# A third seven-product unit in the gate/up chunks of a macaron hybrid layer, with two low parts formed by an adding DMA

## The reference, cut to what matters

```python
def _swiglu_ffn(x, norm_g, w_gate, w_up, w_down):
    h = _rmsnorm(x, norm_g)
    return (jax.nn.silu(h @ w_gate) * (h @ w_up)) @ w_down

h = h + 0.5 * _swiglu_ffn(h, ffn1_norm[l], ffn1_w_gate[l], ffn1_w_up[l], ffn1_w_down[l])
...
h = h + 0.5 * _swiglu_ffn(h, ffn2_norm[l], ffn2_w_gate[l], ffn2_w_up[l], ffn2_w_down[l])
```

## Time and profile before

| | |
|---|---|
| three runs | 2593.53, 2599.84 and 2605.59 us |
| median | 2599.84 us |
| span of the profiled execution | 2591.4 us |
| TensorE busy in the span | 2562.1 us, 99% |
| VectorE, ScalarE, GpSimd busy | 75%, 52%, 7% |
| mean of DMA share and rate | 67% of 16 engines, 212 GB/s |

### The profile page before, as it was taken

The page is one execution under the profiler, slowest core; times in us unless marked ns, Lnnn a source line. Parts: engine busy times, 40 slices in busy tenths (PEclk is TensorE's granted clock), DMA queues, the critical chain, the costliest instruction groups (busy, mean ns, idle before and its releaser), DMA issues.

```text
span 2591.4 us, 34224 instructions
## 1 busy us (share of the span) xinstructions
PE 2562.1 (99%) x13659; PEld 2103.4 (81%) x13659; DVE 1954.8 (75%) x2311; ACT 1339.8 (52%) x1568; POOL 189.2 (7%) x346
## 2 busy tenths in 40 slices
PE   8999999999999999999999999999999999999998
PEld 7888888888888777878788888888888888888887
DVE  6888888887767796959666766555668888888876
ACT  5555555555556366446455544433455455555554
POOL 2000000000000011010001112000100000000000
PEclk9999999999999999999999999999999999999999
DMA  6767676667776575656488779643767677766655
GB/s 213 232 210 242 210 236 218 217 208 228 216 210 195 184 228 159 179 165 181 146 280 257 252 245 281 201 155 130 239 190 230 222 226 225 227 219 218 210 201 175
DMA packets 278576, 548.21 MB, mean 212 GB/s; under 512 B 25020, under 2 KB 35424, under 8 KB 278032
## 3 DMA queue, kind: packets, MB, share of 16 engines
q1 hardware_dynamic: 253904, 478.60, 58.3%
q0 software_dynamic: 24192, 66.89, 8.8%
q10 hardware_dynamic: 320, 0.53, 0.1%
HBM read 508.15 MB, written 37.77 MB: 211 GB/s over the span
## 4 chain that ended last, share of the span: by engine, by line
PE 86%; DVE 8%; ACT 3%; DMA 2%; issue 1%; POOL 0%; SPq 0%; DVEq 0%; ACTq 0%; POOLq 0%
PE pp L794 14%; PE pp L795 14%; PE pp L796 14%; PE pp L415 11%; PE pp L416 11%; PE pp L417 11%; DVE wlo L376 2%; PE pa L794 1%; PE pb L796 1%; PE pb L795 1%; PE pb L794 1%; PE pa L795 1%; PE pa L796 1%; ACT whi L371 1%; DMA raw<-in_ffn_w_up 1%
## 5 line engine op out<-in xcount | busy, mean ns | idle before, releaser
L376 DVE TENSOR_TENSOR wlo<-raw,whi 128x1024 fp32r<-128x1024 f32 (+1 forms) x764 | 919.6, 1216 | 345.9 <-ACT whi L371 326.2
L371 ACT ACTIVATE whi<-raw 128x1024 fp32r<-128x1024 f32 (+1 forms) x764 | 798.0, 1053 | 626.5 <-PE pp L417 438.1
L794 PE MATMUL pp<-whi,xhi 128*128 128x512 f32 x1040 | 404.6, 389 | 0.0
L795 PE MATMUL pp<-whi,xlo 128*128 128x512 f32 x1040 | 404.6, 389 | 0.0
L796 PE MATMUL pp<-wlo,xhi 128*128 128x512 f32 x1040 | 404.6, 389 | 0.0
L415 PE MATMUL pp<-whi,xhi 128*128 128x512 f32 (+1 forms) x928 | 370.6, 399 | 0.7 <-DVE xlo L533 0.7
L417 PE MATMUL pp<-wlo,xhi 128*128 128x512 f32 (+1 forms) x928 | 359.6, 388 | 0.1
L416 PE MATMUL pp<-whi,xlo 128*128 128x512 f32 (+1 forms) x928 | 359.6, 387 | 0.0
L847 ACT ACTIVATE whi<-tw 128x1024 fp32r<-128x1024 f32 x124 | 131.6, 1062 | 276.3 <-PE pp L796 131.6
L794 PEld LDWEIGHTS pp<-whi,xhi 128*128 128x128 f32 x1040 | 195.2, 188 | 40.7
L796 PEld LDWEIGHTS pp<-wlo,xhi 128*128 128x128 f32 x1040 | 195.2, 188 | 40.6
(11 more groups left out here) (528 smaller groups left out, 3669.7 us busy)
## 6 DMA issues: line engine op xcount, KB each, us to landing
raw<-in_ffn_w_gate SPq DMA_DIRECT2D x176, 512.0 KB, 4.3
raw<-in_ffn_w_up SPq DMA_DIRECT2D x176, 512.0 KB, 4.7
raw<-in_ffn_w_down SPq DMA_DIRECT2D x176, 512.0 KB, 4.6
raw<-in_w_in SPq DMA_DIRECT2D x144, 512.0 KB, 4.3
hid_dram<-hid_t POOLq DMA_DIRECT2D x43, 512.0 KB, 5.0
xq<-hid_dram POOLq DMA_DIRECT2D x156, 128.0 KB, 3.8
raw<-in_w_lift SPq DMA_DIRECT2D x32, 512.0 KB, 5.9
raw<-in_w_out SPq DMA_DIRECT2D x32, 512.0 KB, 5.1
```

What stands on the lines that cost most here:

```text
L371: nc.scalar.activation(whi[:, s, :, 0:width], raw[:, r % RING, :, 0:width], ACT.Copy).then_inc(whi_ready, 1)
L376: nc.vector.tensor_tensor(wlo[:, s, :, 0:width], raw[:, r % RING, :, 0:width], whi[:, s, :, 0:width].bitcast(F32), ALU.subtract).then_inc( ...
L794: nc.tensor.matmul(out, a_hi, whi[:, s, block, :], start=start, stop=False)
L795: nc.tensor.matmul(out, a_lo, whi[:, s, block, :], start=False, stop=False)
```

## The change

`GU_UNITS, GU_AFTER` becomes a table for each chunk, `GU_PLAN`. Chunks 1 to 9 get three units instead of two (row blocks 6, 7 and 5, behind t = 1, 3 and 5), so `na` is 5 instead of 6 and there are 10 plain slots instead of 12. Chunk 10 keeps two units behind t = 1 and 5. The third field names plain slots whose low part VectorE no longer writes (t = 1 and 9; in chunk 10 t = 1, 5 and 9): ScalarE writes the negated weights' copy, rounded as `whi` is, to `wlo` (`negate_hi`), and POOL then issues a DMA which reads the weights from DRAM a second time and adds them onto `wlo` (`move_lo`). TensorE waits for the landing of that DMA (`wait_moved`). The sums of activations that a third unit needs are formed once for f1 and once for f2 during chunk 0 (`whole_x`, `xs_third`). Three semaphores are merged with others to make room for two new ones.

```diff
-GU_UNITS, GU_AFTER = (6, 7), (1, 5)
+GU_PLAN = {i: ((6, 7, 5), (1, 3, 5), (1, 9)) for i in range(1, NFC - 1)}
+GU_PLAN[NFC - 1] = ((6, 7), (1, 5), (1, 5, 9))
...
+def copied_at(units, after):
+
+    return max(KT // SK - len(units), after[-1] + 1)
...
         def raw_free(sp, r):
             if r >= RING:
-                sp.wait_ge(wlo_ready, freed_by[r - RING] + 1)
+                last = freed_by[r - RING]
+                if last in lo_moved:
+                    sp.wait_ge(sem("acts_ready"), ACTS[negated_by[last]])
+                else:
+                    sp.wait_ge(wlo_ready, last + 1)
...
+        def negate_hi(act, w):
+
+            r = raw_of[w]
+            nc.scalar.activation(wlo[:, w % RING, :, :], raw[:, r % RING, :, :], ACT.Copy, scale=-1.0).then_inc(sem("acts_ready"), 1)
+
+        def move_lo(pool, w, source):
+
+            pool.wait_ge(sem("acts_ready"), ACTS[negated_by[w]])
+            nc.gpsimd.dma_start(wlo[:, w % RING, :, :], source, accum_op=ALU.add).then_inc(low_landed(lo_moved[w])[0], 16)
...
-        def hidden_turns(pool, tag):
+        def hidden_turns(pool, tag, w_gate, w_up):
             pool.wait_ge(sem("sums_ready"), SUMS[tag, "x"])
-            for i in range(NFC):
-                hidden_out(pool, tag, i)
+            for i in SEVEN:
+                plain, by_dma = prods[tag + "gu"][2 * i]["pair"]["plain"], GU_PLAN[i][2]
+                for t in by_dma:
+                    pr, j, w, _ = plain[t]
+                    weights = w_gate if pr is prods[tag + "gu"][2 * i] else w_up
+                    move_lo(pool, w, weights[j * SK * P:(j + 1) * SK * P, i * CW:(i + 1) * CW].rearrange("(k p) n -> p k n", p=P))
+                    if t == by_dma[0]:
+                        hidden_out(pool, tag, i - 1)
+            hidden_out(pool, tag, NFC - 1)
...
-            pe.wait_ge(wlo_ready, n + 1)
+            if n in lo_moved:
+                wait_moved(pe, n)
+            else:
+                pe.wait_ge(wlo_ready, n + 1)
...
+                if j == 7:
+                    forms_hi(act, xs_third[:, :, :, :], xshi_third[:, :, :, :], (tag, "x", "third"))
...
                     split_hi(act, w, 0)
-                    if t in GU_AFTER:
-                        unit_act(act, pair, GU_AFTER.index(t), (tag, "gu", i))
-                    if t == pair["na"]:
+                    if w in lo_moved:
+                        negate_hi(act, w)
+                    if t in pair["after"]:
+                        unit_act(act, pair, pair["after"].index(t), (tag, "gu", i))
+                    if t == copied_at(pair["units"], pair["after"]):
...
+                if j == 6:
+                    dve.wait_ge(hi_ready, turns[tag + "norm"][1] + 3)
+                    dve.wait_ge(x_ready, turns[tag + "norm"][1] + 3)
+                    link(dve, v.tensor_tensor(whole_x[:, :, :], xhi[:, 10:12, :].bitcast(F32), xlo[:, 10:12, :].bitcast(F32), ALU.add))
+                    forms(dve, whole_x, xs_third, (tag, "x", "third"))
...
-                    split_lo(dve, w, 0)
+                    if w not in lo_moved:
+                        split_lo(dve, w, 0)
...
-                    if t == pair["na"] + 5:
+                    if t == min(pair["na"] + 5, 2 * pair["na"] - 1):
...
-            pe.wait_ge(consts_ready, 1)
+            pe.wait_ge(ident_ready, 2)
```

More of the change, by code:

```diff
@@ L136, in plan @@
     state = dict(p=0, slot=0, raw=0, t=0, s=0, n=0, d=0, freed=[0, 0])
-    raw_of, freed_by = {}, {}
+    raw_of, freed_by, lo_moved = {}, {}, {}
     last = [None, None]
@@ L153, in unit_slots, with pair_slots @@
         return w, r
-    def pair_slots(a, b, units, after):
+    def pair_slots(a, b, units, after, by_dma=()):
         js = [j for j in range(a["ns"]) if j not in units]
@@ L160, in pair_slots @@
             pair["plain"].append((pr, j, *plain_slot()))
+            if t in by_dma:
+                w = pair["plain"][-1][2]
+                lo_moved[w] = len(lo_moved)
             if t < len(js):
@@ L204, in ffn @@
         turned(tag + "act", NFC, by_pe=0)
-        products(tag + "gu", 2 * NFC, [KT], ups=nats[tag + "act"], seven=lambda i: (GU_UNITS, GU_AFTER) if i in SEVEN else None)
+        products(tag + "gu", 2 * NFC, [KT], ups=nats[tag + "act"], seven=lambda i: GU_PLAN.get(i))
         products(tag + "dn", NDC, [FT], seven=lambda q: (DN_UNITS[tag][q], DN_AFTER[tag][q]))
@@ L226, in plan @@
     ffn("f2")
-    return prods, turns, nats, moved, raw_of, freed_by
+    return prods, turns, nats, moved, raw_of, freed_by, lo_moved
+def copied_at(units, after):
+    return max(KT // SK - len(units), after[-1] + 1)
 def count_marks():
@@ L233, in count_marks @@
     for tag in ("f1", "f2"):
-        sums.append((tag, "x"))
-        acts.append((tag, "x"))
-        banks.append((tag, "x"))
+        for marks in (sums, acts, banks):
+            marks += [(tag, "x"), (tag, "x", "third")]
         for i in SEVEN:
-            for u in GU_UNITS:
-                sums += [(tag, "gu", i, u, step) for step in (1, 2, 3)]
-            acts += [(tag, "gu", i, "copied"), (tag, "gu", i, "gate")]
+            units, after, by_dma = GU_PLAN[i]
+            na = KT // SK - len(units)
+            sums += [(tag, "gu", i, u, step) for u in units for step in (1, 2, 3)]
+            for t in range(2 * na):
+                if t in by_dma:
+                    acts.append((tag, "gu", i, "negated", t))
+                if t == copied_at(units, after):
+                    acts.append((tag, "gu", i, "copied"))
+                if t == na + 4:
+                    acts.append((tag, "gu", i, "gate"))
             banks.append((tag, "gu", i))
@@ L256, in build @@
 def build(nc, A):
-    prods, turns, nats, moved, raw_of, freed_by = plan()
+    prods, turns, nats, moved, raw_of, freed_by, lo_moved = plan()
     SUMS, ACTS, BANKS = count_marks()
+    negated_by = {prods[tag + "gu"][2 * i]["pair"]["plain"][t][2]: (tag, "gu", i, "negated", t)
+                  for tag in ("f1", "f2") for i in SEVEN for t in GU_PLAN[i][2]}
     with ExitStack() as ctx:
@@ L921, in ffn_pe @@
                     plain_pe(pe, pair, t, (xhi, xlo))
-                    if t in GU_AFTER:
-                        n = GU_AFTER.index(t)
+                    if t in pair["after"]:
+                        n = pair["after"].index(t)
                         if n == 0:
-                            pe.wait_ge(sem("banks_free"), BANKS[tag, "x"] if i == SEVEN[0] else BANKS[tag, "gu", i - 1])
-                        unit_pe(pe, pair, n, (xhi, xlo), (xshi, xslo), n)
+                            pe.wait_ge(sem("banks_free"), BANKS[tag, "x", "third"] if i == SEVEN[0] else BANKS[tag, "gu", i - 1])
+                        if n < 2:
+                            unit_pe(pe, pair, n, (xhi, xlo), (xshi, xslo), n)
+                        else:
+                            unit_pe(pe, pair, n, (xhi, xlo), (xshi_third, xslo_third), 0)
             pe.wait_ge(x_ready, s0 + NFC - 1)
@@ L1060, in ffn_dve @@
                 for t, (_, _, w, _) in enumerate(pair["plain"]):
-                    split_lo(dve, w, 0)
+                    if w not in lo_moved:
+                        split_lo(dve, w, 0)
                     if t == 3:
                         nat_turn(dve, None, nats[tag + "act"] + i - 1)
-                    if t in GU_AFTER:
-                        n = GU_AFTER.index(t)
+                    if t in pair["after"]:
+                        n = pair["after"].index(t)
                         if n == 0 and i == SEVEN[0]:
-                            dve.wait_ge(sem("banks_free"), BANKS[tag, "x"])
+                            dve.wait_ge(sem("banks_free"), BANKS[tag, "x", "third"])
                         unit_dve(dve, pair, n, (tag, "gu", i), between=(lambda: gated(i - 1)) if n == 0 else None)
```

35 lines of the change are left out of this document (23 added, 12 removed).

## The result

The changed kernel takes **2788.72 us** (median; 2788.32 to 2794.16), the kernel before 2597.57 in the same measurement: a ratio of **1.074** (95% interval 1.072 to 1.076), or +191 us. The forecast was +55, with a range up to 2700. The direction was right; the size was not, and the time lies outside the range.

What follows compares the result with a forecast made beforehand. TensorE, busy 99% of the span, was taken as the bound. Matmuls removed -12.2, boundaries +50.4, chunk 10 +15.0 and four other waits +2.0 gave +55 on 2599.8: 2655 us, 8-in-10 range 2606 to 2700.

Steps and rivals of the forecast that it cites:

- 54 matmuls fewer: Chunks 1 to 9 of f1 and f2: 183 matmuls instead of 186 each, -12.2 us if TensorE stays gapless.
- the 18 boundaries: From t = 9 of chunks 1 to 9 to the next t = 1: TensorE waits 2.8 us each, +50.4 us.
- chunk 10, t = 5: Adding DMA queued on POOL behind chunk 9's turn: TensorE waits 7.5 us, twice, +15.0 us.
- the other four: t = 1 of chunk 1 and t = 9 of chunk 10, in f1 and f2: 0.5 us each, +2.0 us.
- the chain from E over silu and two copies: From a chunk's last unit ending on TensorE to the next chunk's t = 1 negation: ready 10.15 us later.
- POOL's queue in chunk 10: POOL is busy with the hidden turn's loads until 459.28; TensorE reaches t = 5 at 457.73, waiting 7.5 us.
- Part 2: VectorE and ScalarE in a gate/up chunk: busy 37.5 and 26.4 us of 41.5, so both keep up.
- What is L?: Adding DMA's time from issue to landing, estimated from plain transfers: 5.8 us, bounds 3.3 and 7.8.
- slow adding: Rival: the adding DMA's second read makes landing take 7.8 us; +103 us, 2703 us; chance 0.10.
- Part 4: more transfers: Two more 512 KB reads a chunk may delay loads before units: taken as 0, up to 0.5 us a chunk, +9.
- it fits: VectorE's 37.5 us of work in a 41.5 us chunk leaves 4.0 us idle instead of 6.4.
- VectorE becomes the bound: Rival: VectorE's 6.4 us idle stays beside 37.5 of work, chunks take 43.9 us; 2646 us; chance 0.13.

Runs made afterwards that it cites:

- the busy wait: Changed kernel with 20 matmuls into a free PSUM bank before TensorE's wait at t = 9 in chunks 1 to 9: 2763.66 us, ratio 1.063.
- the units behind 1, 5 and 7: Changed kernel with no slot moved, every low part on VectorE, three units behind t = 1, 5 and 7 instead of 1, 3 and 5: 2695.12 us, ratio 1.039.
- free moves: Changed kernel without negations and adding DMAs, the moved slots' low part left out: 2624.42 us, ratio 1.010.
- half the bytes: Changed kernel with no moves, every low part on VectorE; gate/up loads in chunks 1 to 9 fetch 256 KB instead of 512: 2606.63 us, ratio 1.004.

## Why the prediction was right and wrong

The 195.2 us of the profiled execution, against the terms of the sum:

| term | predicted | measured |
|---|---|---|
| 54 matmuls fewer | -12.2 | -12.2 (count as forecast) |
| the 18 boundaries | +50.4, at t = 1 | +87.4, at t = 9 (4.1 to 6.0 each) |
| chunk 10, t = 5 | +15.0 | +14.8 |
| the other four | +2.0 | +13.0 (1.92, 2.71, 3.47, 4.91) |
| half clock behind waits | no term | +41.5 (46.1 less 4.6) |
| third unit (VectorE, loads), and what surrounds the waits | 0, up to 9 | the remaining 50.7 |

*Right.* TensorE without slack, so that every lateness shows; the mechanism, a DMA behind ScalarE's negation that lands too late; the chain from E over silu and two copies (E + 10.0 for E + 10.15), which makes the wait of t = 1 when that move stands alone; POOL's queue in chunk 10, where L happened to be 6.1 (534.54 to 540.68) and so close to the 5.8 taken: that the price of this term came out is luck, its mechanism is not. One working of Part 2 is misread without effect: 464.61 to 465.99 less the waiting is not 1.14; the steps that give it are 465.99 to 467.13 and 470.97 to 472.11.

*First step that failed: "What is L?"* It was put at 5.8 with 7.8 as the upper bound, from POOL's plain transfers. The adding DMA takes 8.6, outside both. The plain copy at the same place takes 6.1, so the nearest rows were good for a plain transfer, and the addition brings 2.5 us on top. Midway between two plain rows left no room for an operation that does more. The rows for the upper bound were also the short ones: the same trace has other loads of 512 KB by POOL (KB each, median us to landing), of other layouts and issued in pairs,

```profile
ga<-proj POOLq DMA_DIRECT2D x2, 512.0 KB, 8.1
gb<-proj POOLq DMA_DIRECT2D x2, 512.0 KB, 9.7
```

and a bound taken from them, 9.7, would have held 8.6. With L = 8.6 the prediction's own formulas would have given 18 x 5.6 + 2 x 10.3 + 4 x 3.3 - 12.2 = +122. So the size of L explains 67 of the 140 us by which the forecast was short; the rest lies in the next two steps. The Trainium skill's estimate of 3.2 us ("DMA: Bandwidth & Descriptors", "Anatomy of one DMA") agrees neither with the 8.6 nor with the 6.1. What the skill says of another adding transfer ("Collectives: The Full Stack", "The bandwidth ceiling": two source reads, half the rate) is borne out by the time of the packets: the queue q0 had 8.8% of the span before, 13.0% in the changed kernel and 11.0% without the addition, so 42 transfers cost 134 and 72 us of the 16 engines, a factor of 1.9. The landing grew 1.4 times only. That rival, slow adding, had a chance of 0.10, and its price ended at 7.8.

*Second: no term for the clock.* The sum priced a wait at its own length. Each of the 21 waits over 4 us in the gate/up chunks is followed by 5 to 12 steps at half speed; in all the half-speed steps add 41 us, about 0.36 us for each us that TensorE waits for a DMA. The experiment with the busy wait shows that the standing still is the cause, and the units behind 1, 5 and 7 show that no adding DMA is needed for it.

*Third: "Part 4: more transfers", and with it "it fits" in Part 2.* VectorE was measured by its busy time in a chunk, which was right (37.8 of 49.5 us; 37.5 forecast), but the loads that VectorE waits for before a unit were noted ("Somewhat later loads can hold up VectorE before a unit") and priced at 0 to 0.5 us a chunk. Without the moves three units cost 52 + 12 = 64 us over 18 chunks, 3.6 us each, with free moves 27 + 12 = 39, 2.2 each. The rival "VectorE becomes the bound" had 2646 us with chunk 10's 15, and was nearer to the truth as a part of the answer than as an alternative to it; half the bytes show that the loads, not VectorE's work, set most of it (43 of the 64 us came back).

*Fourth: the place.* The forecast put 2 to 3 us near t = 1 and 1 to 2 at t = 9. At t = 9 the cover was taken as 4.2 to 4.8 us; at the boundary shown it is 3.5 (253.83 to 257.30), because the load of the slot before was 1.22 us late. With L of 8.0 there the wait comes out at 8.4 - 3.5 = 4.9, and 4.71 was measured.

*What stays open.* Of the remaining 50.7 us, 17 are TensorE's waits for VectorE at units (18.3 less 1.2) and some 5 other waits. Some 28 are busy time beyond clock and count. The starts of the matmuls divide most of it. A wait costs more than its idle time: the last matmul before it counts as busy for its whole 0.39 us in place of the step of 0.23, and the first one behind it starts the next 0.34 us later, or 0.59 where the clock has fallen. The 24 waits for the adding DMA bring 12 us in this way and the waits for VectorE 6 to 7; some 10 in single longer steps stay open. Less the 12, the remainder is 39 us, as much as three units with free moves lost to the count, so it fits the third unit's own price.

No version run here beats the kernel before.

## What to carry to other kernels

Where TensorE has no gap, a gain counted in matmuls must be set against how early its inputs are, unit by unit: an engine's busy share doesn't tell that. A DMA that replaces a vector pass puts its whole landing time on the path of a ring with three slots of cover, and three short slots (8.2 us) don't cover a negation and 8.6 us. When a row for the operation doesn't exist, the upper bound has to come from the slowest rows of its size and from what it does more, and a wait of some us is priced with the slower matmuls behind it.

## What the runs showed of the hardware

- An adding DMA of 512 KB from DRAM onto SBUF took 8.6 us from issue to landing (5.9 to 10.6), the plain one at the same place 6.1 (5.1 to 8.1); issuing it held POOL for 1.22 us in place of 0.71, and the packets of all 42 took 134 us of the 16 engines in place of 72, 1.9 times the time.
- Waits of TensorE of 4.1 to 7.4 us were each followed by 5 to 12 matmul steps at half speed (the granted clock was 0.60 and 0.55 in the stretch shown). Of shorter ones some were (1.92 us: 8 such steps) and some not (2.71 us: none). With 20 matmuls in the place of the wait at t = 9 the half-speed steps fell from 232 to 73.
- Loads of 256 KB landed in 2.7 and 2.9 us (medians of gate and up) where those of 512 KB took 4.2 and 4.8 with three units: half the bytes, on DMA engines that were also less busy (a share of 0.46 in place of 0.67 from 100 to 500 us), took about 0.6 of the time.
